# An expert's first bias by four broadcast transfers into one of two buffers, in place of a selecting matmul and an eviction

## The reference, cut to what matters

```python
def expert_block(args):
    idx, wt, e = args
    xb = h_pad[idx]
    u = xb @ w1[e] + b1[e]                    # w1[e]: 1024 x 2048, b1[e]: 2048
    y = clamped_swiglu(u) @ w2[e] + b2[e]     # w2[e]: 1024 x 1024
    return y.astype(jnp.float32) * wt[:, None]
```

## Time and profile before

| | us |
|---|---|
| median of 3 timed runs | 1527.55 |
| lowest and highest of them | 1525.8, 1531.04 |
| the profiled execution | 1541.51 |
| its span, first to last instruction | 1539.5 |
| mean granted TensorE clock in it | 0.89 |
| PE busy | 1247.8 (81%) |
| DVE, ACT, GpSimd busy | 405.4, 219.3, 281.8 |
| moved by DMA | 464.22 MB |

### The profile page before, as it was taken

One profiled execution on the slowest core, in us unless ns is written; L12 is line 12 of the kernel. 1 busy time (PEld: TensorE's weight loads), 2 busy tenths in 40 slices (PEclk: granted clock), 3 DMA queues, 4 the chain that ended last, 5 costly groups with the idle time before them and its releaser, 6 DMA issues.

```text
span 1539.5 us, 28706 instructions
## 1 busy us (share of the span) xinstructions
PE 1247.8 (81%) x9039; PEld 433.3 (28%) x9040; DVE 405.4 (26%) x826; ACT 219.3 (14%) x482; POOL 281.8 (18%) x431
## 2 busy tenths in 40 slices
PE   3796799444899899988675899997699989999961
PEld 1342345321233233322111233322132223322320
DVE  2111323511223222222110222221032222222317
ACT  2103443200010111110100111111011111100101
POOL 4041000021022212221110121221021211211212
PEclk9797899567999999998876899998799999999975
DMA  9509351419955958899999993559999998899354
GB/s 302 221 2 380 137 218 42 177 63 417 416 215 204 420 228 335 343 393 420 421 419 421 419 420 136 210 217 419 420 378 398 390 419 333 330 420 420 145 196 195
DMA packets 77917, 464.22 MB, mean 302 GB/s; under 512 B 11967, under 2 KB 12071, under 8 KB 29761
## 3 DMA queue, kind: packets, MB, share of 16 engines
q1 hardware_dynamic: 49280, 314.72, 50.5%
q10 hardware_dynamic: 17520, 126.12, 19.9%
q0 software_dynamic: 11088, 22.99, 4.5%
HBM read 454.34 MB, written 16.91 MB: 306 GB/s over the span
## 4 chain that ended last, share of the span: by engine, by line
PE 67%; DMA 17%; DVE 5%; SPq 5%; issue 3%; ACT 2%; POOLq 1%; POOL 1%; ACTq 0%; DVEq 0%
PE bank L1347 32%; PE bank L1375 17%; DMA W<-in_expert_w 11%; PE bank L1253 5%; SPq L366 4%; DMA W<-in_w_ada 4%; PE bank L1299 4%; PE bank L1356 2%; PE bank L1426 2%; PE bank L1221 1%; PE bank L1335 1%; DVE W L1183 1%; DVE OV L1105 1%; PE bank L1269 1%; DMA OV<-h_rows,src_cur 1%
## 5 line engine op out<-in xcount | busy, mean ns | idle before, releaser
L1347 PE MATMUL bank<-W,OV 128*32 128x512 f32 x5056 | 574.1, 607 | 48.2 <-DMA W<-in_expert_w 37.8
L1375 PE MATMUL bank<-W,OV 128*32 128x512 f32 x2528 | 325.9, 661 | 45.9 <-ACT OV L779 22.7
L1347 PEld LDWEIGHTS bank<-W,OV 128*32 128x32 f32 x5056 | 158.4, 111 | 438.6 <-issue 378.2
L1105 DVE TENSOR_TENSOR OV<-bank,OV 128x512 f32<-128x512 f32 x79 | 54.6, 692 | 491.7 <-PE bank L1347 486.2
L1375 PEld LDWEIGHTS bank<-W,OV 128*32 128x32 f32 x2528 | 84.7, 118 | 232.2 <-issue 193.2
L1118 DVE COPY OV<-bank 64x512 f32<-64x512 f32 x79 | 54.7, 693 | 305.0 <-PE bank L1375 305.0
L562 POOL DMA_INDIRECT OV<-h_rows,src_cur x104 | 106.0, 1019 | 62.0 <-POOL src_cur L557 42.6
L557 POOL COPY src_cur<-OV 128x2 int32 (+1 forms) x52 | 11.6, 223 | 493.2 <-PE bank L1335 493.2
L774 ACT ACTIVATE OV<-OV 128x256 f32<-128x256 f32 x79 | 35.1, 444 | 463.0 <-DVE OV L1107 403.0
L1356 PE MATMUL bank<-ident,store 128*128 128x128 f32 x216 | 48.9, 315 | 48.7 <-DVE store L1113 43.8
L1253 PE MATMUL bank<-W 128*128 128x512 f32 x192 | 85.7, 606 | 1.1 <-ACT W L683 1.0
(11 more groups left out here) (228 smaller groups left out, 693.4 us busy)
## 6 DMA issues: line engine op xcount, KB each, us to landing
W<-in_expert_w SPq DMA_DIRECT2D x252, 1024.0 KB
W<-in_expert_w ACTq DMA_DIRECT2D x120, 1024.0 KB
W<-in_w_ada SPq DMA_DIRECT2D x24, 1024.0 KB, 7.7
W<-y_rows SPq DMA_DIRECT2D x4, 2048.0 KB, 14.7
W<-in_w_in SPq DMA_DIRECT2D x3, 2048.0 KB, 12.3
W<-in_w_out SPq DMA_DIRECT2D x1, 4096.0 KB, 20.5
store<-in_x SPq DMA_DIRECT2D x4, 512.0 KB, 5.9
h_rows<-W POOLq DMA_DIRECT2D x4, 512.0 KB, 3.4
```

What stands on the lines that cost most here:

```text
L1105: TTo(u_sb[:, hf, :], bank[hf][:, :], b1_cur, ALU.add).then_inc(u_ok[hf], 1)
L1347: last = mm(bank[hf][H * j:H * j + H, :], xT[:, hf, k % QM, H * (k // QM):H * (k // QM) + H], W1[:, slot, k, UW * j:UW * j + UW], start=(k ...
L1375: last = mm(bank[4 + hf][H * j:H * j + H, :], gT[:, hf, r, H * c:H * c + H], W2[:, c, r, HW * piece:HW * piece + HW], start=(c == 0), stop ...
```

## The change

`b1_all`, which was the table of all biases, becomes one of two buffers `b1_cur[0]` and `b1_cur[1]`. A new helper `load_b1` fills one with four transfers of 32 partitions x 512, each reading 2 KB of the expert's row 32 times (64 KB written, 0.26 MB for the four). ACT issues those of expert 0 at the start, in place of its single load. In the loop SP issues them for expert `e` between the loads of tile 0 and tile 1 of `W1[e]`, after waits for `u_ok[0]` and `u_ok[1]`: DVE must have made all its adds for expert `e - 2`. The selecting matmul, the eviction, the `select` of DVE, the constants and their semaphores are gone; DVE waits for the landing (`b1_in[slot]`) instead.

```diff
+        def load_b1(engine, e, slot):
+            for j in range(J):
+                engine.dma_start(b1_cur[slot][H * j:H * j + H, :],
+                                 expert_b1[0][bass.ds(e, 1), UW * j:UW * j + UW].to_broadcast([H, UW]))\
+                    .then_inc(b1_in[slot], 16)
...
             sp.wait_ge(idx_ok, 1)
+            sp.wait_ge(b1_in[0], 16 * J)
             with sp.If(load > 0):
+                load_b1(sp, 1, 1)
                 for k in range(HALF, KT):
                     load_w1(sp, 1, 1, k)
...
                             load_w1(sp, e, slot, k)
+                            if k == 0:
+                                sp.wait_ge(u_ok[0], s + 1)
+                                apart(sp)
+                                sp.wait_ge(u_ok[1], f + 1)
+                                apart(sp)
+                                load_b1(sp, e, slot)
...
-            act.dma_start(b1_all[:, :], expert_b1[0].rearrange("e (j c) -> (e j) c", j=J)).then_inc(b1_in, 16)
+            load_b1(act, 0, 0)
...
-                    act.wait_ge(b1_ps, act.snap(biased, min_val=0, max_val=E) + 1)
-                    nc.scalar.activation(b1_cur, b1_bank[:, :], ACT.Copy).then_inc(b1_ok, 1)
...
-                    dve.wait_ge(b1_ok, biased)
+                    dve.wait_ge(b1_in[slot], biased[slot])
...
-                    dve.wait_ge(sel_e_ok, dve.snap(e + 1, min_val=1, max_val=E))
-                    select(bass.ds(e + 1, 1), 1 - slot)
...
-                        pe.wait_ge(sel_e_ok, e + 1)
-                        mm(b1_bank[:, :], sel_e[:, slot, :], b1_all[:, :], start=True, stop=True).then_inc(b1_ps, 1)
```

More of the change, by code:

```diff
@@ L187, in hybrid_layer @@
         y_sb = [take(HW)[0:YP], take(HW)[0:YP]]
-        sel_e = take(2, P)
-        b1_cur = take(UW)
+        b1_cur = [b1_all[:, :], take(UW)]
         y_part = [take(HW)[0:YP], take(HW)[0:YP]]
         take = carver(OV[:, 5888:])
-        same_j = take(P)
-        hot_row = take(E + 1)
         idx = take(2, NQ // 2, 2).bitcast(i32)
@@ L286, in hybrid_layer @@
         w2_in = sems("w2_in", J)
-        b1_in = sem("b1_in")
-        bias_const = sem("bias_const")
-        sel_e_ok = sem("sel_e_ok")
-        b1_ps = sem("b1_ps")
-        b1_ok = sem("b1_ok")
+        b1_in = sems("b1_in", 2)
         x1_stored = sem("x1_stored")
@@ L335, in hybrid_layer @@
         gT_bank = [bank[3], bank[6]]
-        b1_bank = bank[7]
         GELU = 2.0 * (2.0 / 3.141592653589793) ** 0.5
@@ L536, in _ @@
                 .then_inc(route_const, 1)
-            nc.gpsimd.iota(same_j.bitcast(i32), [[-1, J], [0, H]], base=P, channel_multiplier=1).then_inc(bias_const, 1)
-            nc.gpsimd.iota(hot_row.bitcast(i32), [[-J, E + 1]], base=P, channel_multiplier=1).then_inc(bias_const, 1)
             link(nc.gpsimd.memset(upper, 1.0))
@@ L787, in _ @@
             down_step, down_full = act.alloc_register("act_down_step"), act.alloc_register("act_down_full")
-            biased = act.alloc_register("act_biased")
-            for reg in (step, full, turned, down_step, down_full, biased):
+            for reg in (step, full, turned, down_step, down_full):
                 act.reg_mov(reg, 0)
@@ L800, in expert @@
                 with act.If(n_halves > 0):
-                    act.wait_ge(b1_ps, act.snap(biased, min_val=0, max_val=E) + 1)
-                    nc.scalar.activation(b1_cur, b1_bank[:, :], ACT.Copy).then_inc(b1_ok, 1)
-                    act.reg_add(biased, biased, 1)
                     with act.If(n_full > 0):
@@ L1096, in _, with activate @@
             dve.wait_ge(idx_ok, 1)
-            def activate(hf, n, k):
+            def activate(slot, hf, n, k):
                 gate, lin = u_parts(hf)[:, :, 0], u_parts(hf)[:, :, 1]
                 if hf == 0:
-                    dve.wait_ge(b1_ok, biased)
+                    dve.wait_ge(b1_in[slot], biased[slot])
                 dve.wait_ge(u_ps[hf], n + 2)
-                TTo(u_sb[:, hf, :], bank[hf][:, :], b1_cur, ALU.add).then_inc(u_ok[hf], 1)
+                TTo(u_sb[:, hf, :], bank[hf][:, :], b1_cur[slot], ALU.add).then_inc(u_ok[hf], 1)
                 dve.wait_ge(u_ok[hf], n + 2)
@@ L1122, in finish @@
                 TTo(y_sb[hf], bank[4 + hf][0:YP, :], y_part[hf], ALU.add).then_inc(y_ok[hf], 1)
-            def select(e, slot):
-                TS(sel_e[:, slot, :], same_j, hot_row[:, e], None, ALU.mult).then_inc(sel_e_ok, 1)
-            select(slice(0, 1), 0)
             dve.wait_ge(x1_stored, 16 * TT)
@@ L1133, in _ @@
             parts = dve.alloc_register("dve_parts")
-            biased = dve.alloc_register("dve_biased")
-            for reg in (step, full, down_step, down_full, parts, biased):
+            biased = [dve.alloc_register(f"dve_biased{v}") for v in range(2)]
+            for reg in (step, full, down_step, down_full, parts, biased[0], biased[1]):
                 dve.reg_mov(reg, 0)
+            first_halves = dve.value_load(counts[0:1, 1, 0:1], min_val=0, max_val=T // H)
+            with dve.If(first_halves < 1):
+                dve.reg_add(biased[0], biased[0], 16 * J)
             with dve.Fori(0, E // 2) as pair:
@@ L1141, in _ @@
                     n_full = dve.value_load(counts[0:1, 2, bass.ds(e, 1)], min_val=0, max_val=T // (2 * H))
-                    dve.wait_ge(sel_e_ok, dve.snap(e + 1, min_val=1, max_val=E))
-                    select(bass.ds(e + 1, 1), 1 - slot)
                     with dve.If(n_halves > 0):
-                        dve.reg_add(biased, biased, 1)
+                        dve.reg_add(biased[slot], biased[slot], 16 * J)
                         with dve.If(n_full > 0):
@@ L1149, in _ @@
                                 f = dve.snap(full, min_val=0, max_val=STEPS_MAX)
-                                activate(0, s, dve.snap(2 * k, min_val=0, max_val=T // H - 1))
-                                activate(1, f, dve.snap(2 * k + 1, min_val=0, max_val=T // H - 1))
+                                activate(slot, 0, s, dve.snap(2 * k, min_val=0, max_val=T // H - 1))
+                                activate(slot, 1, f, dve.snap(2 * k + 1, min_val=0, max_val=T // H - 1))
                                 dve.reg_add(full, full, 1)
@@ L1155, in _ @@
                             s = dve.snap(step, min_val=0, max_val=STEPS_MAX)
-                            activate(0, s, dve.snap(n_halves & (T // H - 2), min_val=0, max_val=T // H - 2))
+                            activate(slot, 0, s, dve.snap(n_halves & (T // H - 2), min_val=0, max_val=T // H - 2))
                             dve.reg_add(step, step, 1)
@@ L1391, in _ @@
             pe.wait_ge(counts_ok, 4)
-            pe.wait_ge(b1_in, 16)
             step, full = pe.alloc_register("pe_step"), pe.alloc_register("pe_full")
```

5 lines of the change are left out of this document (removed).

## The result

| | before | after |
|---|---|---|
| median, same chip, 4 runs each | 1529.3 us | 1558.41 us |
| lowest and highest | 1525.8, 1534.59 | 1554.18, 1562.64 |
| profiled execution | 1541.51 | 1556.44 |
| ratio after / before, 95% interval | | 1.0187 [1.0143, 1.0231] |

The change makes the kernel slower by 1.4 to 2.3%, some 29 us. The forecast was no change at 1527 us, and the range ended at 1537. The direction is that of rivals 2 and 3, and the size is beyond both together.

The account below looks back on a forecast made before the run. Experts were taken to alternate between DMA-bound weight loading and PE. 17.4 us saved against 10.9 of holes, 5.2 of bytes and 1.1 of expert 18's head given back: -0.2 us, 1527 us, range 1514 to 1537.

Parts of the forecast that it names:

- rival 2: A third hole at expert 20, 1029 to 1035 us, adds 5.9 us: 1533 us; chance 0.17.
- Rival 3: Broadcast transfers on SP's queue cost 1.6 us per expert, not 0.65, 7.6 us more: 1535 us; chance 0.12, including both slow rivals.
- The heads: Bias matmul removed between last down and first up matmul: 1.06 us at 18 of 31 experts, less overlap, saves 17.4 us.
- PE stretches: Times that end with PE: the bias matmul costs there, a later transfer does not if it lands in time.
- full stretch: Weights for experts 2 and 3, 10 to 15, 18 to 21: bytes set the end, PE savings buy nothing.
- The waits: SP holds back tiles 1 to 7 of W1: idle-DMA holes of 5.7 us at expert 2, 5.2 at expert 10.
- Rival 1: Holes at experts 2 and 10 cost nothing, made up later as W2 transfers move forward: 1516 us; chance 0.26.
- all other refills in full stretches find a queue with several tiles still waiting: 0: Delayed W1 loads in DMA-bound times, apart from experts 2, 10 and 20, were taken to cost 0.
- PE stretches: 0: Delayed W1 loads where PE is the limit cost 0: at expert 25, 29 us of slack against 6 of delay.
- The bytes: Four bias transfers, 0.26 MB, cost 0.65 us per expert, counted at 8 experts where DMA is full: 5.2 us.
- The clock and the first stretch: Expert 2's hole and expert 3's bias add 6.4 us; named wrong if expert 3's stall kept PE's clock lower longer.
- The Trainium skill's rule: Transfers under 64 KB pay mostly overhead: 8.6 us per expert, 69 us for 8, near 1592 us; trace was said to disagree.

Follow-up runs that it names:

- gain_only: Changed kernel without the bias transfers and without SP's waits for them; every expert adds expert 0's bias: 1525.43 us, ratio 0.9909.
- wait_only: Changed kernel without the bias transfers, but SP still waits between tile 0 and tile 1; every expert adds expert 0's bias: 1538.36 us, ratio 1.0007.
- plain_first_b: Changed kernel with one 128 x 512 transfer of plain rows (not the expert's) replacing the four, same place and waits; second run of plain_first: 1544.27 us, ratio 1.0068.
- wait_only_b: wait_only run again, as base of three other kernels on one chip: 1537.8 us, ratio 1.0004.
- one_repeat_first: Changed kernel with one transfer reading one 2 KB row 128 times in place of the four, same place and waits: 1546.1 us, ratio 1.0075.
- plain_first: Changed kernel with one 128 x 512 transfer of plain rows (not the expert's) in place of the four, same place and waits: 1542.75 us, ratio 1.0047.
- expanded_last: Changed kernel with all biases spread out once in DRAM early; each expert's bias is one plain 128 x 512 load behind tile 7: 1517.21 us, ratio 0.9938.

## Why the prediction was wrong, point by point

**The heads: right in kind, too high in size.** 17.4 us foreseen with bounds of 11.7 and 19.1; gain_only gives 10.1 by the medians, 14.0 (10 to 18) by the ratio. At experts of more than two halves in PE stretches it is 1.1 us each, as foreseen. What the sum missed is that a head saved ahead of a full stretch was put at 0, and that the removal cost 2.5 us in the first stage.

**The waits: nearly right in size, partly by luck.** 10.9 us foreseen, 12.9 by the medians. The price shows in the first and third stage, as foreseen. In the first stage it is the hole: the DMA engines are idle 4 to 6 us more than in gain_only. In the third it is a hole only in part: about 3 us of idle engines against 5.2 foreseen, and much of the rest goes with `W2` that moves ahead of `W1`. Rival 1 named such a forward move as what would make the holes cost nothing; here it is a part of the cost. Rival 1 fell, as did the hole of rival 2 (the fourth stage is no longer in wait_only than in gain_only). What failed is the item "all other refills in full stretches find a queue with several tiles still waiting: 0". It looked only at loads issued inside full stretches. Expert 9's load is issued just ahead of one, and its hole (69 GB/s at 627 to 633) leaves the bytes to be moved later. In "PE stretches: 0", too, something was missing. I had named it among what would make the prediction wrong: `W1`'s burst lies closer to `W2`'s loads. At expert 25, two halves, `down` in the changed kernel:

```profile
1281.12 5.35 PE L1367 MATMUL bank<-W,OV 128*32 128x512 f32 x24
1287.56 2.78 PE L1367 MATMUL bank<-W,OV 128*32 128x512 f32 x24 [1.09 <-DMA W<-in_expert_w]
```

and in the kernel before, traced again:

```profile
1249.78 6.62 PE L1375 MATMUL bank<-W,OV 128*32 128x512 f32 x48
```

The 48 matmuls take 6.62 us there, and 9.22 from the first's start to the last's end here, with a wait of 1.09 us for `W2` in the middle and PE slower before it (granted clock 0.54 from 1281 to 1287, against 0.80 over the 6.62 us). By the last stage of the two wait-only kernels against gain_only this is worth 2 to 3 us in all; nothing finer can be said, since the two traces of before are 9.5 us apart in that stage.

**The bytes: this step failed.** "So 0.65 us (upper bound of this kind 0.8) per expert" took the mean of the whole queue per MB. That held for one wide transfer: third stage, plain_first_b less wait_only_b, 4.2 us for six biases, 0.7 each. For the change's four it is 224.0 - 213.1 = 10.9 us, 1.8 each, or 1.5 against the other trace of wait_only. Rival 3 had 1.6 per expert, and so about the right price, for the wrong reason (repeated rows), and I gave it 0.12. I had no row for a transfer into 32 partitions, took the nearest (whole tiles of 128 partitions), and did not take that as a lower bound only. Repeated or not, such a transfer also slows the 8 KB packets beside it, which the sum had nothing for.

**The clock and the first stretch.** At the stall of expert 3 PE was on its lower clock: granted 0.50, that is 1.2 GHz, at 397 to 407 after matmuls of 8 with 3 us of waiting between them. The 48 matmuls that follow the last wait take 7.99 us, against 7.05 before: 0.9 us. But it is not the longer stall that did it: the lower clock lasts 3.4 us past the last wait in the kernel before, 5.4 here, and 5.6 in gain_only, whose last wait ends only 1.3 us later in the stage than that of before. The first stage came out 14.9 us longer, 6.4 foreseen. By the runs the removal alone is 2.5 of it, the waits are 4 to 6 (wait_only, wait_only_b over gain_only), one transfer 3 to 5 more, four narrow ones another 2 to 3. That a first transfer costs 3 to 5 us there, with two biases' bytes worth 1.3, goes with `W2` again: before the last wait ends its queue has moved 8.39 MB in plain_first_b, 8.18 in wait_only_b and 7.72 in wait_only. The sum had taken it that the bytes ahead of PE's last tile stay the same, but for the biases. What sets the share of the two queues no run here varies alone.

**The sum by the runs,** each term from the medians of two kernels of one group: matmul -10.1 (first group), waits +12.9 (first), bytes of one transfer +4.4 (first) or +6.5 (fourth), four instead of one +3.5 for the number and +8.0 for the partitions (fourth), repeated rows +3.0, not told from 0 (second). That is +21.7 to +23.8; the changed kernel measured +22.0 in the second group and +29.1 in the result. The interval of the result begins at 1.0143, which is +22, so the two measurements do not contradict each other; what the other 7 us are, these runs don't tell. Against the prediction's -0.2 the largest error is the bytes: 5.2 foreseen, 15.9 to 18.0 measured without the repetition.

**The Trainium skill's rule in the prediction** ("DMA: Bandwidth & Descriptors", sections "Rules for kernel authors" and "Anatomy of one DMA": small transfers pay mostly overhead; an estimate of 8.6 us per expert by its fit) had the sign, and the trace's disagreement holds on the size: 1.5 to 1.8 us per expert beside a full queue, a fifth of it. The page gives the fit for transfers issued from GpSimd, and these are SP's. That I weighed this rule and not the one on ports was the choice that cost most.

**Open.** Repeated rows cost 3 us by the medians, not told from 0. Why the kernel before has two forms of its last stage in its two traces (314.8 and 305.3 us) I don't know; at experts of two halves the gap from `up` to `down` is 4.2 us in the first trace and 3.0 in the second.

## What to carry to other kernels

Where all DMA engines are busy, cost an added transfer by its form and not by its bytes alone: the transfers here that used few engines (outermost dimension 4) or 32 neighbouring partitions slowed what ran beside them, and the others did not. Behind a wait in an in-order issuing queue, count every load that now leaves late, also those issued ahead of a full stretch, since their bytes are moved in it, and see what another queue moves meanwhile: those bytes may come ahead of the ones that are awaited. And before a small matmul is traded for transfers, look for a place where its engine waits anyway.

## What the hardware showed that I had not expected

- 64 KB writes into 32 neighbouring partitions, 0.26 MB among some 13 MB, lower the rate of a full queue from 419 to 407 GB/s; the same writes to every fourth partition do not.
- A transfer of 128 rows whose source has 4 as its outermost dimension leaves 4 completion packets instead of 16, and costs 3.8 us per expert (third stage) more than a plain one of the same bytes and packet size; behind tile 7 it is dear too (1.0251 against 0.9938 for the plain one of expanded_last).
- Reading one 2 KB row 128 times costs some 3 us per run over reading 128 rows, not told from 0 (one_repeat_first 1546.1 us and 1.0075, plain_first 1542.75 and 1.0047, in different groups, intervals overlapping).
- Taking work from PE ahead of a full stretch can lengthen it: with the matmul gone (gain_only) 1.84 MB more of `W2` came through ahead of the awaited `W1`, and the stage took 2.5 us longer.
